# Last projections by token halves, modulation sums as rows of one bank, fp32r row spreading and a shuffle for the rotary swap in a one-layer hybrid mLSTM and attention kernel

## What is computed

```
h = rms_norm(x, n_pre[0]) * (1 + sc0) + sh0
x = x + 0.5 * g0 * rms_norm(swiglu(h, f_in[0], f_out[0]), n_post[0])
h = rms_norm(x, n_pre[1]) * (1 + sc1) + sh1
y, st = token_mixer(h, *mix_w, ctx)        # mLSTM (8 heads) and attention (16 q / 4 kv heads), merged by gates, one output projection
x = x + g1 * rms_norm(y, n_post[1])
h = rms_norm(x, n_pre[2]) * (1 + sc2) + sh2
x = x + 0.5 * g2 * rms_norm(swiglu(h, f_in[1], f_out[1]), n_post[2])
```

## Time and profile before

| | |
|---|---|
| median of 3 runs | 1914.7 us (1912.04 to 1916.28) |
| the profiled execution | 1912.14 us, its span 1910.2 us |
| TensorE busy | 1837.8 us, 96% |
| VectorE busy | 952.2 us, 50% |
| ScalarE busy | 666.8 us, 35% |
| chain of work that ended last | TensorE 88%, VectorE 5%, ScalarE 4%, issue 2% |
| DMA | 178.47 MB, mean 93 GB/s |

### The profile page before, as it was taken

How to read it: one execution, slowest core, us unless ns; L and a number is a source line. 1 busy time by engine, 2 the same in 40 slices (tenths; PEclk the granted TensorE clock), 3 DMA queues, 4 the chain that set the end, 5 groups by cost and what they waited for, 6 DMA issues and landing times.

```text
span 1910.2 us, 31603 instructions
## 1 busy us (share of the span) xinstructions
PE 1837.8 (96%) x12928; PEld 1761.7 (92%) x12928; DVE 952.2 (50%) x1576; ACT 666.8 (35%) x1134; POOL 0.2 (0%) x4
## 2 busy tenths in 40 slices
PE   6899999999979999999999999989989999999996
PEld 6899999999959998889989888879969999999996
DVE  4665565656366224444436788865372222232235
ACT  3422222112365222433334545443572222221233
POOL 0000000000000000000000000000000000000000
PEclk9999999999999999999999999989989999999998
DMA  7444444543222224232243211102302222222221
GB/s 300 152 155 126 156 130 137 154 124 112 63 89 89 67 67 101 74 89 72 73 132 109 66 38 54 38 19 78 133 25 86 73 71 78 77 77 69 72 58 55
DMA packets 52300, 178.47 MB, mean 93 GB/s; under 512 B 8521, under 2 KB 11099, under 8 KB 51427
## 3 DMA queue, kind: packets, MB, share of 16 engines
q1 hardware_dynamic: 52195, 176.97, 29.2%
HBM read 162.40 MB, written 13.90 MB: 92 GB/s over the span
## 4 chain that ended last, share of the span: by engine, by line
PE 88%; DVE 5%; ACT 4%; issue 2%; DMA 0%; SPq 0%; DVEq 0%; ACTq 0%
PE psum L499 22%; PE psum L501 22%; PE psum L500 22%; PE psum L902 2%; PE psum L892 2%; PE psum L867 2%; PE psum L604 1%; PE psum L593 1%; PE psum L536 1%; PE psum L538 1%; PE psum L537 1%; PE psum L756 1%; PE psum L950 1%; PE psum L952 1%; PE psum L951 1%
## 5 line engine op out<-in xcount | busy, mean ns | idle before, releaser
L499 PE MATMUL psum<-h_hi,whi 128*128 128x320 f32 x2160 | 677.9, 314 | 3.6 <-ACT gf L1178 1.8
L501 PE MATMUL psum<-h_hi,wlo 128*128 128x320 f32 x2160 | 668.0, 309 | 0.0
L500 PE MATMUL psum<-h_lo,whi 128*128 128x320 f32 x2160 | 667.9, 309 | 0.0
L1388 DVE TENSOR_TENSOR wlo<-raw,whi 128x1024 fp32r<-128x1024 f32 x207 | 252.9, 1222 | 740.9 <-ACT whi L999 740.8
L499 PEld LDWEIGHTS psum<-h_hi,whi 128*128 128x128 f32 x2160 | 406.1, 188 | 10.4 <-issue 7.4
L500 PEld LDWEIGHTS psum<-h_lo,whi 128*128 128x128 f32 x2160 | 406.4, 188 | 1.9 <-issue 1.9
L501 PEld LDWEIGHTS psum<-h_hi,wlo 128*128 128x128 f32 x2160 | 406.1, 188 | 0.0
L999 ACT CAST whi<-raw 128x1024 fp32r<-128x1024 f32 x207 | 216.1, 1044 | 379.4 <-PE psum L501 364.1
L499 PE MATMUL psum<-g_hi,whi 128*128 128x320 f32 x608 | 188.4, 310 | 1.0 <-DVE g_lo L1597 1.0
L500 PE MATMUL psum<-g_lo,whi 128*128 128x320 f32 x608 | 187.9, 309 | 0.0
L501 PE MATMUL psum<-g_hi,wlo 128*128 128x320 f32 x608 | 187.9, 309 | 0.0
(11 more groups left out here) (296 smaller groups left out, 2384.3 us busy)
## 6 DMA issues: line engine op xcount, KB each, us to landing
raw<-in_w_ffn_in SPq DMA_DIRECT2D x88, 512.0 KB, 3.5
raw<-in_w_mix SPq DMA_DIRECT2D x77, 512.0 KB, 3.8
mw<-in_w_mod SPq DMA_DIRECT2D x28, 768.0 KB, 4.5
raw<-in_w_ffn_out SPq DMA_DIRECT2D x32, 512.0 KB, 3.5
mw<-in_w_mod SPq DMA_DIRECT2D x4, 2048.0 KB, 19.6
gate<-gate_keep SPq DMA_DIRECT2D x24, 320.0 KB, 4.5
mw<-in_w_mod SPq DMA_DIRECT2D x14, 512.0 KB, 3.6
gate_keep<-gate SPq DMA_DIRECT2D x20, 320.0 KB, 4.5
```

Of the source, the lines that this page charges most:

```text
L499: mm(out, whi[t.slot][:, k, :], hi[:, k, cols], start=(k == 0), stop=False)
L500: mm(out, whi[t.slot][:, k, :], lo[:, k, cols], start=False, stop=False)
L501: last = mm(out, wlo[t.slot][:, k, :], hi[:, k, cols], start=False, stop=(k == nk - 1))
L1388: tt((lo or wlo[t.slot])[:, :, :], raw[t.raw][:, :, :], (hi or whi[t.slot])[:, :, :].bitcast(F32), ALU.subtract).then_inc(raw_free, 1)
```

## The change

1. `last_tiles`: all eight tiles run for tokens 0:320, then all for 320:640 in the order 2,3,4,5,0,1,6,7 (`SECOND`). The weights of tiles 2 to 5 stay in new places (`held`), those of 6 and 7 in `xhi`, `xlo`. Only the nk slabs in use are split. The next norm's squares and sums for half 0 stand between the tiles of half 1, and the norm has two steps: VectorE multiplies x by scale and root at once (one instruction for each group of tokens), ScalarE adds the shift and writes `h_hi`, VectorE adds the shift and subtracts for `h_lo`. `first_four` takes the place of `first_two`: tiles 0 to 3 for half 0, with the sums of half 1 among them, then all four for half 1; tiles 2 and 3 use banks 4 to 7.
2. Modulation: `pick` holds a column of ones at the place of a row; for each group two matmuls of 512 columns add the sums as two rows of bank 7, which stays open over all 14; at the end one copy, four transposes and four additions.
3. Spreads: the rows are split into two fp32r parts, in partitions 0 to 7 and 32 to 39, and spread by fp32r matmuls over 40 rows with a 0/1 selector that is now made on the chip.
4. Rotary: the swap is a VectorE stream shuffle; the matmul is gone and the sine table carries the sign.
5. At the end of FFN 1 the transposes of token blocks 0 and 1 stand between tiles of half 1.

In the diff the pieces stand in the order placement, TensorE, ScalarE, VectorE; removed lines are mostly left out, as the functions before are printed above.

```diff
+        whole = KC * P * 4
+        held = [[at(f"held{u}_{n}", [P, KC, P], F32R, h_at + (u - 2) // 2 * KC * row + (u % 2 * 2 + n) * whole)
+                 for n in range(2)] for u in range(2, 6)]
...
+            def half_tile(l, i, u, base, h, nk, hi, lo, ready=None, first=0):
+                t, w = Tile(base + i), Tile(base + u)
+                wh, wl = weights(l, u, base)
+                if h == 0:
+                    pe.wait_ge(raw_free, w.n + 1 + RAWS)
...
                 out = half_out(t.slot, h)
...
+                for k in range(nk):
+                    if ready is not None:
+                        pe.wait_ge(ready, first + k + 1)
                     mm(out, wh[:, k, :], hi[:, k, HCOLS[h]], start=(k == 0), stop=False)
                     mm(out, wh[:, k, :], lo[:, k, HCOLS[h]], start=False, stop=False)
                     last = mm(out, wl[:, k, :], hi[:, k, HCOLS[h]], start=False, stop=(k == nk - 1))
...
+            def last_tiles(l, base, nk, hi, lo, ready, first):
+                for u in range(KC):
+                    half_tile(l, u, u, base, 0, nk, hi, lo, ready if u == 0 else None, first)
+                for i, u in enumerate(SECOND):
+                    half_tile(l, i, u, base, 1, nk, hi, lo)
+                    if i == 0:
+                        half_stats_y(l, 0)
+                    if l < 2 and i in (2, 3, 4):
+                        half_stats(l, 0, (range(0, 2), range(2, 5), range(5, KC))[i - 2])
+                    if l == 2 and i >= KC - 3 and i < KC - 1:
+                        turn_out(i - (KC - 3))
...
             def sum_mod(n):
                 pe.wait_ge(mod_mul, 2 * KC * (n + 1))
-                pe.wait_ge(mod_ev, n + 1)
-                sum_products(7).then_inc(mod_done, 1)
+                for g in range(2):
+                    last = mm(psum[0:MOD_ROWS, 7, :], pick[:, g * MOD_ROWS:(g + 1) * MOD_ROWS], macc[:, g, :],
+                              start=False,
+                              stop=isinstance(n, int) and n == MOD_LATER - 1 and g == 1)
+                last.then_inc(mod_done, 1)
...
+            def first_four(l, base):
+                t = [Tile(base + u) for u in range(4)]
                 for h in range(2):
...
+                    for u in range(2):
+                        if h == 0:
+                            pe.wait_ge(raw_free, t[u].n + 1 + RAWS)
+                            pe.wait_ge(h0_ev, KC * l + KC - 1 + u)
+                        else:
+                            pe.wait_ge(ev[t[u].slot], t[u].pair)
+                    for k in range(KC):
+                        for u in range(2):
+                            last = first_half(l, base, u, h, range(k, k + 1), u == 0)
+                            if h == 1 and k == KC - 1:
+                                last.then_inc(tile_done, 1)
+                    for u in range(2, 4):
+                        if h == 0:
+                            pe.wait_ge(raw_free, t[u].n + 1 + RAWS)
+                        last = first_half(l, base, u, h, range(KC), False)
+                        if h == 0:
+                            half_stats(l, 1, range(4 * u - 8, 4 * u - 4))
+                        else:
+                            last.then_inc(tile_done, 1)
             def ffn(f, base):
...
-                    last = mm(bc[:, :, hh, :], sel1[:, 2 * j + hh, :], nm[:, :, tok], start=True, stop=True)
+                    last = mm(bc[:, :, hh, :], sel1[:, 2 * j + hh, :], nm_pair[:, :, tok], start=True, stop=True)
...
                 if n >= 1:
                     pe.wait_ge(qk_rb, n)
-                    pe.wait_ge(rope, n)
                 for h in range(2):
-                    mm(half_out(2, h), ones_h, sq[n % 2][:, h * HALF:(h + 1) * HALF], start=True, stop=True)
-                mm(psum[:, 6, :], swap, qk(n)[:, TP:N], start=True, stop=True).then_inc(qk_st, 1)
+                    last = mm(half_out(2, h), ones_h, sq[n % 2][:, h * HALF:(h + 1) * HALF], start=True, stop=True)
...
+            def high_half(l, h, ks):
+                for k in ks:
+                    act.wait_ge(half_t, n_half(l, h, k))
                     for g, cols in HGROUPS[h]:
...
+                        last = fn(h_hi[:, k, cols], sa[k % 2][:, cols], ACT.Identity,
+                                  bias=mod[:, 3 * (l + 1) * KC + k, g:g + 1])
+                    last.then_inc(half_hi, 1)
...
+            def last_tiles(l, base, nxt, nk):
+                w = [Tile(base + u) for u in range(KC)]
...
+                for i in range(KC):
+                    u = i + 2
+                    if u == 6:
...
+                    if u < KC:
+                        split(w[u], weights(l, u, base)[0], w[0].n + 2, nk)
+                    square_y(l, i, 0, base)
+                second(0)
                 root_y(l, 0)
...
+                square_x(l, 0, range(1, 3))
+                second(2)
+                square_x(l, 0, range(3, 6))
+                second(3)
+                square_x(l, 0, range(6, KC))
+                second(4)
+                first_split(0)
+                root_x(l, 0)
+                high_half(l, 0, range(0, 2))
+                second(5)
+                first_split(1)
+                high_half(l, 0, range(2, 4))
+                second(6)
+                high_half(l, 0, range(4, 6))
+                second(7)
+                high_half(l, 0, range(6, KC))
                 root_y(l, 1)
...
-                    square_x(l, 1, range(KC))
...
+                first_split(3)
+                square_x(l, 1, range(3, KC))
+                root_x(l, 1)
+                high_half(l, 1, range(KC))
...
                 last.then_inc(ev[t.slot], 1)
...
+                if l == L_GATE + 1:
+                    split(t.plus(4), None, t.n + 3)
+                elif l > 3:
                     split(t.plus(2))
...
+                if l == L_MK + 3:
+                    act.wait_ge(nm_zero, 2)
+                    copy(nm_pair[0:H, :, :], gb[:, :, :]).then_inc(nm_hi, 1)
+                if l == L_MK + 4:
+                    copy(t_pair[0:H, :, :], t1[:, :, :]).then_inc(t_hi, 1)
...
+            def half_normed(l, h, ks):
                 def low(k):
...
+                    dve.wait_ge(half_hi, n_half(l, h, k))
+                    for g, cols in HGROUPS[h]:
+                        last = stt(h_lo[:, k, cols], sa[k % 2][:, cols], mod[:, 3 * (l + 1) * KC + k, g:g + 1],
+                                   h_hi[:, k, cols].bitcast(F32), ALU.add, ALU.subtract)
+                    last.then_inc(h_rdy, 1)
+                if ks.start == 0:
+                    dve.wait_ge(rx, 2 * l + h + 1)
+                for k in ks:
                     if k >= 2:
...
+                        dve.wait_ge(h_rdy, KC + n_half(l, h, k - 2))
+                    for g, cols in HGROUPS[h]:
+                        last = stt(sa[k % 2][:, cols], x[:, k, cols], pre_s[:, l + 1, k, g:g + 1], rb[:, cols],
+                                   ALU.mult, ALU.mult)
+                    last.then_inc(half_t, 1)
                     if k >= 1:
...
+                    t = Tile(base + i)
+                    u = SECOND[i] if h else i
+                    dve.wait_ge(*((tile_done, t.n + 3) if h else (h0_done, KC * l + i + 1)))
+                    tt(y[:, u, HCOLS[h]], y[:, u, HCOLS[h]], half_out(t.slot, h), ALU.add).then_inc(ev[t.slot] if h else h0_ev, 1)
...
+                for i in range(KC):
+                    if i + 2 < KC:
+                        split(w[i + 2], weights(l, i + 2, base), nk)
+                    take(i, 0)
+                    if i >= 2:
+                        add_y_square(l, i - 1, 0)
...
+                residual(l, 0, range(0, 1))
+                take(1, 1)
+                residual(l, 0, range(1, 3))
+                add_y_square(l, 1, 1)
+                take(2, 1)
+                residual(l, 0, range(3, 6))
+                add_y_square(l, 2, 1)
+                take(3, 1)
+                residual(l, 0, range(6, KC))
+                add_y_square(l, 3, 1)
+                take(4, 1)
+                add_y_square(l, 4, 1)
+                if nxt is None:
+                    for i in (5, 6, 7):
+                        take(i, 1)
+                        add_y_square(l, i, 1) if i < 7 else None
+                    residual(l, 1, range(KC))
+                    return
+                first_split(0)
+                half_normed(l, 0, range(0, 2))
+                take(5, 1)
+                half_normed(l, 0, range(2, 3))
+                add_y_square(l, 5, 1)
+                first_split(1)
+                half_normed(l, 0, range(3, 4))
                 take(6, 1)
...
+                half_normed(l, 0, range(4, 5))
+                add_y_square(l, 6, 1)
+                half_normed(l, 0, range(5, 6))
                 take(7, 1)
...
+                half_normed(l, 0, range(6, KC))
+                residual(l, 1, range(0, 3))
+                first_split(2)
+                residual(l, 1, range(3, 6))
```

(26 more changed lines are left out.)

489 lines of the change are left out of this document (231 added, 258 removed).

## The result

The changed kernel takes 1891.08 us (median of four runs, 1890.41 to 1893.12) against 1914.59 us before: the ratio is 0.988, 95% interval 0.9863 to 0.9897. That is 23.5 us gained where 34.7 were forecast, inside the range and 11 us above the predicted 1880. So 14.3 us have to be found.

A forecast was written before the change was run, and what follows sets the result against it. TensorE, busy 96% of the span, was taken as the bound. From 1912.14 us, -18.7 - 6.3 + 0.6 - 7.2 - 1.6 + 0 = -33.2 gave 1878.9, stated as 1880 since the median was 2.6 higher; range 1861 to 1895.

The forecast's parts named there:

- the projections' waits: New TensorE waits in the three last projections; 10 us of the range was allowed for them.
- Spreads, c above 0: Row spreads in sixteen mLSTM units: one-pass fp32r matmuls gain 1.02 us each, 16.3 us together.
- the change of kind: Row spreads: 0.12 us left for the change between fp32r and fp32 matmuls.
- Spreads, c = 0: Row spreads in the four mLSTM units with two spreads each: 0.97 us becomes 0.36, gain 2.4 us together.
- Rotary: Swap matmul removed: 0.86 us a tile, 6.9 for eight, less one 0.6 us shuffle before attention; gain 6.3 us.
- Modulation: Modulation sums: two 512-column matmuls cost the same as eight of 128; with four transposes, loss 0.6 us.
- l = 0: FFN 0's last projection through the gate turn: half tiles with new waits, gain 1.6 us.
- l = 1: Output projection and the stage after it: 104.0 us instead of 111.2, gain 7.2 us.
- l = 2: FFN 1's last projection to the end: 54.3 against 53.9 us, with the end's clock gain counted as 0.
- Rival A: Halves hide the norms, so waits in rounds, before y sums and behind the Ln don't arise: 1862 us; chance 0.20.
- Rival B: Row spreads run at the fp32 pace: 1899 us; chance 0.13, shared with smaller gains.
- Rival C: Granted clock falls over first passes of last projections at l = 0 and 2: 1915 us or slower; chance 0.03.

The follow-up runs named there:

- a_nosig: Changed kernel with the sigmoid of output gates 4 to 7, and so ScalarE's table loads, left out: units with c = 0 start 9.0 us apart (one execution).
- a_busy: Changed kernel plus matmuls with overwritten results in front of four kinds of TensorE waits: 1889.77 us, ratio 0.9878.

## Why the prediction was right, and where its sum was off

The time lay in the range and the sign was right; six of the ten terms were off by no more than 1.7 us. What earned it are the spreads with c above 0 and the rotary tiles, 25.1 us of the gain. That the rest stayed in the range is in part luck: 10 us of it were meant for the projections' waits, and they covered misses of 3.3, 3.9 and 2.4 us in terms that had bounds near 0 to 2.

- **Spreads, c above 0:** forecast 16.3, measured 18.0. The 0.12 us that I had left for the change of kind is not paid. It was the upper bound of the range. (For all twenty units that bound is 18.7 and twenty times 0.12, 21.1, not the 21.5 that I wrote.)
- **Spreads, c = 0:** forecast a gain of 2.4, measured a loss of 1.5. The step that failed is the first one, that TensorE sets the pace there. ScalarE's ring does (`a_nosig`): where the clock stays up, the four units take 37.5 us with the new spreads as with the old, a gain of 0. The other 1.5 are the clock, which fell once, behind two waits of 0.91 and 1.02 us in unit 1.
- **Rotary:** the 0.86 us a tile were right (7.1 against 6.9). At the start of attention the term was 0.6 and the kernel lost 3.0: two tiles and so two shuffles lie on VectorE's chain, not one, though the second is covered in part (1.0 us for both); each is 0.74 us, not 0.6; and the clock falls behind the wait, which makes about half of it (from the first transpose to the first values 4.6 us instead of 3.1). By the Trainium skill ("VectorE: DVE Perf Modes", The perf-mode tier table) 512 elements would be an estimated 0.6 us; the row at 1042.93 says 0.74.
- **Modulation:** forecast a loss of 0.6, measured 3.9. "Two of 512 have as many columns" holds; that the weight block has another shape than its neighbours costs 0.25 us a round, fourteen times, which my sum had put at nothing without a row for it.
- **l = 0:** forecast a gain of 1.6, measured a loss of 3.7. The waits were nearly right one by one: 2.8 for `g_lo` (2.8 forecast), 2.9 in the first pass (4.3), none at the x sums (0.6), 4.6 at the y sums (4.1), 3.1 for the root (3.4), 4.7 behind the Ln (4.9), 0.5 at `turn_gates` (0.5). Together 18.6 against 20.6. What is missing is mostly the clock: I had added up matmuls at full pace, and behind the four longest of these waits they ran at half of it. `a_busy`, with the clock up, takes 127.5 us for this stretch, so the clock is 3.7 of the 5.3 us. The other 1.6 are waits: with the clock up TensorE is through with the first four tiles 97.2 us after the start of this stretch and tile 4 starts at 103.0, 5.8 us later instead of 4.9; and the first four tiles begin 0.9 us later than in my sum. In the changed kernel slow matmuls stand in the place of these waits, which is why its waits look shorter than forecast.
- **l = 1:** 6.3 against 7.2, with one low stretch of 1.4 us near 1411.
- **l = 2:** -0.7 against 0; the tail behind it is 0.9 longer. The transposes that moved forward had stood in its waits before, so moving them won nothing; why it is longer is not shown. The granted clock is 0.50 from 1878 us to the end, in the kernel before from 1890 to 1897 and again from 1907.5.

Rival A (the halves hide the norms) is out: every wait it would have removed is in the trace. Rival B is out by the pace of the spreads. Rival C was wrong as put, since the clock stays at 1.00 in the first passes with their small holes, but its mechanism was the largest thing that my sum lacked. It belonged into the sum as a price on the waits near 3 us that no other wait follows closely, not into a rival that needs a whole pass. The kernel before showed that price at 575 to 580 us.

How the miss of 14.3 us splits, to 0.2: 3.3 weight shape, 5.3 at l = 0, 3.9 at c = 0, 2.4 at attention, 0.9 + 0.2 at l = 1, l = 2 and the tail, less 1.9 that spreads and rotary brought on top. The forecast was compared with one execution, and two executions of the changed kernel differ by 6.6 us.

## What to carry to other kernels

A wait of TensorE near 3 us costs itself and, most times, another 1 to 1.5 us of half-pace matmuls behind it, unless TensorE would soon have waited again: price each wait that a change adds that way. If it can't be removed, it can be filled with matmuls nobody reads; that kept the clock up in most cases here, while the gain in the median over four runs was too small to tell. The same kernel loses more or less this way from one execution to the next, so a forecast to 2 us can't be judged on one execution. Work taken from the busiest engine is won only where no wait of that engine closes a ring through another, so read what ends its waits for each kind of unit, not the busy share of the stretch. When a stall is moved, look for the chain that ends next before counting the gain, and for the one line of program order that makes a round serial.
